# Eight of 31 convolution taps computed on VectorE instead of GpSimd, in a two-layer trunk

## The reference

```python
def _conv_group(z, conv_w, conv_b, ln_g, ln_b):
    u = z[..., :CONV_CH] * jax.nn.sigmoid(z[..., CONV_CH:])
    u = lax.conv_general_dilated(u, conv_w[:, None, :], window_strides=(1,),
                                 padding=[(CONV_K - 1, 0)], ...
                                 feature_group_count=CONV_CH) + conv_b
    return jax.nn.silu(_layernorm(u, ln_g, ln_b))
```

## Time and profile before

| | us |
|---|---|
| median of 3 runs | 1866.31 |
| lowest, highest | 1865.82, 1869.94 |
| profiled execution | 1865.88 |
| its span in the profile | 1864.0 |

### The profile page before, as it was taken

How to read it: one execution, slowest core, us unless ns; L and a number is a source line. 1 busy time by engine, 2 the same in 40 slices (tenths; PEclk the granted TensorE clock), 3 DMA queues, 4 the chain that set the end, 5 groups by cost and what they waited for, 6 DMA issues and landing times.

```text
span 1864.0 us, 39016 instructions
## 1 busy us (share of the span) xinstructions
PE 1783.0 (96%) x14384; PEld 1735.8 (93%) x14384; DVE 1452.3 (78%) x3027; ACT 837.5 (45%) x1771; POOL 875.0 (47%) x635
## 2 busy tenths in 40 slices
PE   9978899999999899999999788999999999999999
PEld 8966899999999899999989768999999999999998
DVE  2686558895499889999946755688644998999997
ACT  6523441211476545555546225412114776555543
POOL 4895560234143447676437964602341333554540
PEclk9979899999999999999999878999999999999999
DMA  5400345899899899999944002568998997999995
GB/s 197 136 2 2 104 157 192 304 402 391 340 349 339 299 345 415 420 419 412 392 141 155 2 2 91 173 205 315 375 409 304 328 339 279 381 388 391 387 385 188
DMA packets 138648, 505.84 MB, mean 271 GB/s; under 512 B 15392, under 2 KB 15520, under 8 KB 138272
## 3 DMA queue, kind: packets, MB, share of 16 engines
q1 hardware_dynamic: 87840, 319.68, 46.2%
q0 software_dynamic: 50688, 184.57, 26.0%
HBM read 503.14 MB, written 1.05 MB: 270 GB/s over the span
## 4 chain that ended last, share of the span: by engine, by line
PE 69%; DVE 20%; DMA 5%; issue 4%; ACT 2%; SPq 0%; ACTq 0%; POOL 0%; DVEq 0%; POOLq 0%
PE ps L1100 69%; DMA w<-v_c 5%; DVE arena L2164 3%; DVE onehots_i L2096 2%; DVE rows_w L1942 2%; DVE w_lo L2148 1%; DVE x_hi L2140 1%; DVE arena L2117 1%; DVE rows_x L1942 1%; ACT w_hi L789 1%; DVE x L1662 1%; DVE x_lo L1655 1%; DVE arena L1677 1%; DVE arena L1707 1%; DVE onehots_j L1650 0%
## 5 line engine op out<-in xcount | busy, mean ns | idle before, releaser
L1100 PE MATMUL ps<-x_hi,w_hi 128*128 128x352 f32 (+2 forms) x2544 | 721.8, 342 | 20.6 <-DVE x_lo L1655 10.9
L1100 PE MATMUL ps<-x_hi,w_lo 128*128 128x176 f32 (+2 forms) x2544 | 646.8, 254 | 0.0
L1100 PE MATMUL ps<-x,w 128*128 128x176 f32 x4096 | 627.8, 313 | 0.0
L1100 PEld LDWEIGHTS ps<-x,w 128*128 128x128 f32 x4096 | 612.5, 190 | 0.6 <-issue 0.2
L1100 PEld LDWEIGHTS ps<-x_hi,w_hi 128*128 128x128 f32 x2544 | 480.0, 189 | 35.3 <-DVE x_hi L2140 10.1
L1100 PEld LDWEIGHTS ps<-x_hi,w_lo 128*128 128x128 f32 x2544 | 485.7, 191 | 0.0
L789 ACT CAST w_hi<-w 128x1024 fp32r<-128x1024 f32 x318 | 334.2, 1051 | 318.2 <-DMA w<-v_c 234.0
L717 POOL DMA_INDIRECT arena<-v_c,sel x176 | 311.3, 1769 | 226.4 <-DVE arena L2164 199.6
L685 POOL TENSOR_TENSOR w_lo<-w,w_hi 128x1024 fp32r<-128x1024 f32 x90 | 222.4, 2485 | 211.7 <-ACT w_hi L789 211.6
L2148 DVE TENSOR_TENSOR w_lo<-w,w_hi 128x1024 fp32r<-128x1024 f32 x228 | 278.0, 1219 | 32.2 <-ACT w_hi L789 31.6
L717 POOL DMA_INDIRECT rows_w<-ur_c,sel x116 | 120.7, 1040 | 232.5 <-DVE sel L1942 222.7
(11 more groups left out here) (196 smaller groups left out, 1739.5 us busy)
## 6 DMA issues: line engine op xcount, KB each, us to landing
w<-u_c SPq DMA_DIRECT2D x256, 512.0 KB, 5.7
w<-v_c SPq DMA_DIRECT2D x256, 512.0 KB, 6.5
w<-w_c SPq DMA_DIRECT2D x84, 512.0 KB, 3.5
arena<-v_c,sel POOLq DMA_INDIRECT x176, 8.2
arena<-keys_c SPq DMA_DIRECT2D x2, 1024.0 KB, 8.3
arena<-mix_c SPq DMA_DIRECT2D x2, 964.0 KB, 8.8
rows_w<-ur_c,sel POOLq DMA_INDIRECT x116, 7.9
h<-h SPq DMA_DIRECT2D x2, 544.0 KB, 5.0
```

Source lines behind the costliest of these rows:

```text
L1100: return nc.tensor.matmul(out_, lhsT, rhs, start=start, stop=stop, skip_group_check=True)
```

## The change

Of the 31 taps GpSimd computes the first 23. VectorE computes the last eight into `yT`, ahead of the masks of the Gram products: a product for each half for the first of them, and a multiply-add (`scalar_tensor_tensor`) for each half for the seven others. GpSimd adds `yT` to its own sum at the end. Three waits are new: both engines wait for the gated input (`s_cu`), GpSimd's last sum waits for VectorE's taps (`s_tap`), and ScalarE waits for the convolution before it overwrites `yT`.

```diff
+TAPS_DVE = 8
...
                 link(g.memset(cu[:, :, 0:CPAD], 0.0))
-                link(g.tensor_tensor(cu[:, :, CPAD:CPAD + T], z[:, ZCU:ZCU + 2, 1:T + 1], cacc[:, :, :], ALU.mult))
-                for k in range(CONV_K):
+                g.tensor_tensor(cu[:, :, CPAD:CPAD + T], z[:, ZCU:ZCU + 2, 1:T + 1], cacc[:, :, :],
+                                ALU.mult).then_inc(s_cu, 1)
+                pool.wait_ge(s_cu, l + 1)
+                for k in range(CONV_K - TAPS_DVE):
...
                     if k:
-                        ins = g.tensor_tensor(cacc[:, :, :], cacc[:, :, :], ctmp[:, :, :], ALU.add)
-                        link(ins) if k < CONV_K - 1 else ins.then_inc(s_conv, 1)
+                        link(g.tensor_tensor(cacc[:, :, :], cacc[:, :, :], ctmp[:, :, :], ALU.add))
+                pool.wait_ge(s_tap, l + 1)
+                g.tensor_tensor(cacc[:, :, :], cacc[:, :, :], yT[:, :, 0:T], ALU.add).then_inc(s_conv, 1)
                 lows(l, NZ, NPROJ)
...
                 beside()
+                act.wait_ge(s_conv, l + 1)
                 for k, (c0, cn, bank) in enumerate(YB):
...
                 nlev = len(LEVELS) - 1
 
+                dve.wait_ge(s_cu, l + 1)
+                for k in range(CONV_K - TAPS_DVE, CONV_K):
+                    for j in range(2):
+                        tap, weight = cu[:, j, k:k + T], vcol(l, "conv_w", j * CONV_K + k)
+                        if k == CONV_K - TAPS_DVE:
+                            ins = v.tensor_scalar(yT[:, j, 0:T], tap, weight, None, ALU.mult)
+                        else:
+                            ins = v.scalar_tensor_tensor(yT[:, j, 0:T], tap, weight, yT[:, j, 0:T], ALU.mult, ALU.add)
+                        if k == CONV_K - 1 and j == 1:
+                            ins.then_inc(s_tap, 1)
+                        elif j == 0:
+                            ins.then_inc(s_dl, 1)
+                            link.n += 1
+                        else:
+                            link(ins)
+
                 for c in range(NCH):
```

More of the change, by code:

```diff
@@ L546, in trunk @@
         s_conv = sem("conv_done")
+        s_cu = sem("conv_input_gated")
+        s_tap = sem("vector_taps_done")
         s_cm = sem("conv_sums_in_psum")
```

## The result

| | kernel before | changed kernel |
|---|---|---|
| median of the runs | 1866.65 us (5) | 1876.25 us (5) |
| lowest, highest | 1865.82, 1869.94 | 1872.02, 1880.20 |
| profiled execution | 1865.88 us | 1872.93 us |
| its span | 1864.0 us | 1871.1 us |

The changed kernel is slower: ratio 1.0043, interval 1.0022 to 1.0064. The forecast was no measurable difference, 1867.0 us with a range of 1861.4 to 1874.0: wrong, and outside its range. The same kernel, run a second time on another occasion, gave 1877.95 us (12 runs) and a ratio of 1.0052 (1.0035 to 1.0070).

What follows compares the result with a forecast made beforehand. TensorE, busy 96% of the span, was taken as the bound, its mixer-stage waits being for VectorE. Taps + 0.4, first layer - 2.0, second layer + 2.7 gave + 1.1 on 1865.9: 1867.0 us, range 1861.4 to 1874.0.

Steps and rivals of the forecast that it cites:

- The bound: Mixer stages: TensorE waits for VectorE, nothing on the path for the convolution's end; the change acts only through VectorE.
- The taps: VectorE before chunk 0's mask: GpSimd gets in once per pair, 10.5 us, nearly hidden, cost 0.2 us per layer.
- rival 1: VectorE's taps alternate with GpSimd one by one, 15.5 us, mask 5.4 us late per layer: 1877.4 us, chance 0.24.
- The three signs that the prediction named for being wrong: Chunk 0's mask after 91 us, TensorE's chunk 2 Gram product waiting for VectorE, or TensorE's granted clock falling elsewhere.
- GpSimd's end: GpSimd's convolution ends at about 140.2 us instead of 157.14, in the second layer at about 1081.
- The first layer's relief: Softmax of 150 to 154.8 us is free of GpSimd: 2.0 us less, bounds 0 and 2.0.
- the term for this collision: First layer, splits from 140 to 147.5 us: no cost was entered for splits meeting a softmax there.
- The second layer: Splits from 1081 to 1088 us meet the softmax chain: 5.2 us against 2.5, so 2.7 us lost.
- the other bound: Second layer: the splits miss the softmax chain, 2.5 us gained.
- rival 2: Relief in both layers' softmaxes, splits missing the second's chain: - 2.0 - 2.5 = - 4.5, 1861.4 us, chance 0.19.
- The sum: Whole kernel: taps + 0.4, first layer - 2.0, second layer + 2.7, together + 1.1 us, 1867.0 us.
- its mask price: Chunk 0's mask, and so TensorE, 5.4 us late in each layer: + 10.8 us in rival 1.

Runs made afterwards that it cites:

- Experiment 1: Changed kernel with VectorE's eight taps left out altogether, GpSimd making 23: 1872.49 us, ratio 1.0021 to the kernel before.
- Experiment 3: Changed kernel with GpSimd starting its 23 taps only when VectorE's eight are done: 1867.29 us, ratio 0.9990 to the kernel before.
- experiment 6: Changed kernel with VectorE's taps accumulated in PSUM, only the last tap writing `yT`: 1871.76 us, ratio 1.0014 to the kernel before.
- experiment 7: The kernel of experiment 6 with GpSimd's three weight splits moved ahead of its 23 taps: 1867.30 us, ratio 0.9997 to the kernel before.
- experiment 8: Changed kernel with taps accumulated in PSUM and weight splits held until VectorE has copied the solved pairs: 1859.29 us, ratio 0.9953 to the kernel before.
- experiment 5: Changed kernel with GpSimd's weight splits held until VectorE has copied the last solved pairs: 1865.05 us, ratio 0.9982 to the kernel before.
- experiment 2: Changed kernel with GpSimd keeping all 31 taps and VectorE's eight made besides but unused: 1874.04 us, ratio 1.0034 to the kernel before.
- experiment 4: Changed kernel with four taps on VectorE instead of eight, 27 on GpSimd: 1870.57 us, ratio 1.0010 to the kernel before.
- the control of experiment 7: Kernel before, all 31 taps on GpSimd, with the three weight splits moved ahead of the taps: 1867.02 us, ratio 0.9993.

## Why the prediction was wrong

**The bound: right.** Nobody waited for the convolution in any kernel, and the change acted through VectorE alone. Experiment 1 shows it best: eight taps gone and nothing gained.

**The taps: this step failed.** "If it gets in once between two pairs, it does so eight times" gave 10.5 us and a cost of 0.2 per layer. GpSimd got in after every multiply-add, the prediction's rival 1. The 16 took 14.0 us (80.70 to 94.71) instead of rival 1's 15.5, TensorE waited 3.9 us in each layer instead of 5.4: + 7.8 where the sum had + 0.4. The three signs that the prediction named for being wrong all came: the mask at 94.71, TensorE waiting for it, and the clock granted otherwise (0.59 for 0.83 from 95 to 115 us). Experiment 3 shows that the stretch comes from GpSimd (13.26 against 6.62 us), experiments 6 and 7 that for a multiply-add it needs the second operand in SBUF. The evidence that the prediction held against rival 1 was one row, L1832 at 0.48 us, behind an instruction that had itself been held up; a lone pair is no measure for a queue of 16. The Trainium skill's rule ("SBUF — State Buffer", section "SBUF: two separate sides"), which it cited for the rival, fits the multiply-adds: with two SBUF inputs they are stretched, with one they are not. That one engine is locked out for the other's whole instruction is seen on VectorE only: GpSimd's turn of three instructions grew by 0.31 us with three of VectorE's in it. Who is let in next the rule does not say; here the engines alternated.

**GpSimd's end: right within 1.5 us.** Predicted 140.2, measured 138.8 in the first layer (137.45 + 1.34); VectorE's instructions pushed GpSimd back by 1.5 us up to there, not by 3. In the second 1081 was given and it came at 1089.1, in a stage that began 9.65 us late: 1079.4 on the clock of the kernel before, 1.6 early again.

**The first layer's relief: right in size, and only half of the story.** The fourth softmax gained 2.0 us of TensorE's time (its wait 2.23 for 4.24), as forecast; its steps are at 0.16 and 0.76 us as given. What the prediction did not look at is which steps stand at the splits' new place. It checked where they had been and not where they would be: "the three splits run from 140 to 147.5" was followed for the second layer alone. In the first, VectorE was late enough for the third softmax to reach 140.7 us, and the loss was 4.3 us. Experiment 1 shows that on time it fares no better, since then the steps behind the softmax are hit. So the term for this collision was put at nothing without a look: - 2.0 forecast, + 4.3 - 2.0 = + 2.3 measured.

**The second layer: the sign was wrong.** + 2.7 was forecast for a collision; with VectorE late, the splits fell into its idle time, and the softmax was relieved: - 2.5, the other bound (rival 2's half). That the splits missed is luck of the late mask. With the mask in time they hit this softmax, two steps of 2.17 and 2.26 us, 1.6 us lost over the kernel before where 2.7 was forecast (experiment 6). The mechanism that was put here also struck in the first layer, near the predicted size of a step: 2.27 us for one small instruction, twice, against 2.4.

**The sum.** 0.4 - 2.0 + 2.7 = + 1.1 was forecast. By the same terms 7.8 + 2.3 - 2.5 = + 7.6 was measured, of 8.0 in the two stages. Rival 1 had the taps' mechanism right. That its 1877.4 us was also near the time is in part luck: its mask price was too high, and its terms for the splits were wrong in both layers and nearly cancelled.

**What stays open.** The weight-streaming stages last from 829.1 to 833.2 us between the mixer stages and from 732.5 to 737.7 behind them, over all the profiles here; no run isolated why. Why experiment 7 gained nothing where experiment 8 gained 0.47% is shown in part: around the second layer's last softmax TensorE waits 2.16 and 2.04 us against 0.76 and 0.51, 2.9 of the 5.1 us between their second stages (107.2 and 102.1). The rest is open; their profiles also differ in the clock granted in the first stage (0.81 and 0.88), and nothing here sets that apart from its causes. The same holds for the clock everywhere in this document: no run changes it alone.

## What to carry to other kernels

Before moving work to an idle VectorE beside a busy GpSimd, price each instruction with two operands in SBUF at one instruction of GpSimd's, not at its undisturbed time; if one operand can lie in PSUM, the undisturbed time holds. When a change moves an engine's long instructions that nobody waits for, look at what will stand beside them at the new place, in each layer, with the shift that the change itself brings: small steps of a dependent chain pay a whole long instruction each. And an engine's finishing early is no gain if what follows in its queue is then free to run at a worse moment; a wait for an existing semaphore puts it back, and in experiments 5 and 8 it cost nothing that the traces show.

## What the runs showed of the hardware that was not expected

- **Alternation.** 14 multiply-adds of VectorE (128x272, float32, two operands in SBUF) took 13.26, 13.26 and 13.27 us beside GpSimd's convolution (the changed kernel, experiment 2, the changed kernel again), 6.62 us without it. GpSimd's turn grew only from 2.48 to 2.79 us meanwhile, so the loss lies almost wholly with VectorE.
- **One operand in PSUM removes all of it**, on both engines: 5.67 us for 12 beside products and sums, 5.66 with five of them beside a split, and GpSimd's turn 2.49.
- **The size of VectorE's instruction does not matter.** Four elements a partition waited 2.27 us for a split, as did a `tensor_scalar` with a single SBUF operand on the same size (L1723 above, 2.27 us). In the kernel before, a `tensor_scalar` of 272 columns (L1857) took 2.33 us beside a split, and 0.36 with GpSimd idle in the changed one. But the first two taps, of the same kind and size, took 0.79 us together beside the convolution and 0.63 without it: for this kind the wait can be long or short, and no run separated the two. So a single SBUF operand does not protect a `tensor_scalar` as it protects a multiply-add.
- **The clock granted behind the mask differs.** From 95 to 115 us it was 0.83 in the kernel before and in experiment 6, where the mask came in time, and 0.59 in all three profiles with the changed kernel's first layer (the changed kernel twice, experiment 5). But experiment 4 and the control of experiment 7, with their masks in time, also had 0.59, so the wait for the mask is not the only way to it, and it is not shown to be one. The window's rows, before and after (busy us of PE, PEld, DVE, ACT, POOL, then clock, DMA share, GB/s):

```profile
95.00:115.00 20.00, 11.65 (x244) 10.98 (x244) 19.03 (x43) 4.75 (x20) 18.70 (x22) 0.83 0.01 2
```

```profile
95.00:115.00 20.00, 12.71 (x184) 12.03 (x186) 18.57 (x35) 3.34 (x13) 18.64 (x24) 0.59 0.01 2
```

- In experiment 6 the 152 products behind the splits' collision took 15.69 us at a mean clock of 0.54 (143 to 160 us), near the lower of the two levels, 1.2 of 2.4 GHz; in the kernel before the same 152 took 10.12 us. The 5.6 us between them are more than the stall of 3.6 us ahead of them. That the stall brought the lower clock is likely (experiment 1, with such stalls, had 0.60 there, and experiments 7 and 8, without, 1.00 and 0.96), but no run changed the one without the other.
